# Gate projections of two row blocks formed together from seven block products each, in a Griffin-style trunk layer on one Trainium2 core

## The chip, the core and the metric

The kernel runs on one core of one Trainium2 chip. Its five engines run their own instruction streams and wait for each other through semaphores: PE (TensorE, matrix products into PSUM banks), DVE (VectorE), ACT (ScalarE), POOL (GpSimd), and SP (SyncE), which here issues most DMA transfers. The metric is the device time of one execution in microseconds; less is better.

## The reference

One layer over x of 2048 rows and 1024 channels, batch 1, float32 throughout. Only the projection concerns the change; the rest says what follows it.

```python
h = _rmsnorm(x, norm1_g[layer])
proj = jnp.einsum('bsd,de->bse', h, w_in[layer])
(a_q, a_k, a_v, b_q, b_lat, i_q, i_k, i_w, gate_a, gate_b) = _split_cols(proj)
o_a = _mixer_a(...)       # sliding-window attention, 8 heads
o_b = _mixer_b(...)       # indexer scores, top 256 keys per row, attention over them
merged = (jax.nn.sigmoid(gate_a) * jnp.einsum('bse,ed->bsd', o_a, w_branch_a[layer])
          + jax.nn.sigmoid(gate_b) * jnp.einsum('bse,ed->bsd', o_b, w_branch_b[layer]))
x = x + jnp.einsum('bsd,de->bse', merged, w_out[layer])
# then x + SwiGLU(RMSNorm(x)) and a final RMSNorm
```

gate_a and gate_b have 1024 columns each: 16 column tiles of 128, numbered 0 to 15 below.

## The kernel before, in words

The 2048 rows are cut into four row blocks of 512 (`ROWS`, `NB`). The program first projects block 0, then 1, 2 and 3; then it runs, block by block, the attention, the branches, the output projection and the feed-forward part. A **job** is one column tile of one block: eight depth tiles of 128, and for each of them three products, since every float32 operand is held as a high and a low part in the type that PE takes (`three`, L1102: high by high, high by low, low by high). A projection job is thus 24 matmuls of 128x128 by 128x512, summed in one of four PSUM banks that are taken in turn (`take`, L1089). The table `JOBS` (L385) sets the order: per block iq (4 jobs), ikw, lat, av, ak, aq (4), bq (4) and the 16 gate tiles; the list `SECOND` (L386) is the part from av on.

What is done for a job on each engine:

- SP loads its 512 KB of weights into one of two tiles `WRAW` (L861), in the order of `JOBS`. Before the load of job i it waits until POOL has split job i-2, and it issues, at fixed places of the same queue, what has to be written out or loaded meanwhile (`spill` L660, `first_attention` L819).
- POOL splits the weights, half a job (four depth tiles, 128x512) at a time: `WHI` by L1038 and `WLO` by L1040. The half of job i waits until PE is through with job i-2 (L1032), whose `WHI`/`WLO` it overwrites.
- PE runs the job (`job`, L1107).
- ACT and DVE take the bank away. For a gate tile ACT applies the sigmoid and writes the 256 KB to DRAM (L1939, L1941).

Where a new block begins, PE turns the normalised rows (`XN`) into columns, ACT writes their high part `HThi` (L1882) and DVE the low part `HTlo` (L2461), eight columns of 128x512 each; the first four are turned within the last job of the block before, the other four within the first job of the new block.

Beside the jobs run two more things. The indexer's scores: PE makes units of up to 128x1024 in PSUM (`score`, L1253), spread over the jobs from `SECOND`'s sixth on by `score_share` (L593); ACT applies the relu, DVE multiplies and adds (L2447). And the search for block 0's top keys (`search`, L2192): one step per job of `SECOND` in blocks 1 and 2, in which DVE sets thresholds and counts one row tile, and ACT counts another (L1849). The last two gate tiles of block 3 (`HELD`) are run within the first attention. The queries for it (`QA`) are loaded into the place of the indexer's keys, so SP waits for the last score (L834) before it issues that load, just ahead of the load of gate tile 12 of block 3.

The product of seven instead of eight block products is already used for the down projection of the last block (`seven_products`, L1189).

## Time and profile before

| what | us |
|---|---|
| three runs: median (lowest, highest) | 3185.56 (3185.35, 3195.97) |
| the profiled execution's own time | 3185.86 |
| its span in the profile | 3183.9 |
| PE busy, share of the span | 3143.7, 99% |
| POOL busy | 2059.9, 65% |
| DVE busy | 2005.0, 63% |
| ACT busy | 1449.8, 46% |

A busy time is the union of an engine's instructions; matmuls overlap their neighbours in it, so the time that one more matmul costs is the distance between two starts, not the duration of one. The projections take from the start to about 859 us; block 1 begins at 205 us.

### The profile page before, as it was taken

How to read it: one execution, taken by the hardware profiler on the slowest of the kernel's cores; microseconds unless marked ns; L12 is line 12 of the kernel's file. 1: busy time of each engine (PE TensorE's matmuls, PEld its weight loads, DVE VectorE, ACT ScalarE, POOL GpSimd, SP SyncE). 2: the span in 40 equal slices, each digit the busy share in tenths (PEclk: the TensorE clock that was granted, in tenths of full speed). 3: DMA queues.
4: the chain of work that ended last, by engine and by line, in shares of the span. 5: the costliest groups of instructions: out<-in, count | busy, mean ns of one | idle time of the engine just before them, and what ended most of it. 6: DMA issues, size and time to landing. Idle time of an engine off the chain costs nothing.

```text
span 3183.9 us, 44209 instructions
## 1 busy us (share of the span) xinstructions
PE 3143.7 (99%) x15612; PEld 2643.7 (83%) x15612; DVE 2005.0 (63%) x3889; ACT 1449.8 (46%) x2622; POOL 2059.9 (65%) x2185
## 2 busy tenths in 40 slices
PE   9999999999999999999999999999999999999998
PEld 7888888878888888889888888988888789888887
DVE  3235546537565545557666666967868679647757
ACT  3324445435472534337354543846655368431202
POOL 5666666665556666764666676366666932568778
PEclk9999999999999999999999999999999999999999
DMA  5765455355615333331633334163333411444443
GB/s 154 197 168 172 120 150 161 106 158 164 210 35 182 103 106 108 109 133 35 218 103 108 107 111 139 30 213 116 102 108 105 151 62 21 137 160 127 126 127 101
DMA packets 474699, 401.25 MB, mean 126 GB/s; under 512 B 29905, under 2 KB 405969, under 8 KB 473841
## 3 DMA queue, kind: packets, MB, share of 16 engines
q1 hardware_dynamic: 441072, 342.68, 35.9%
q10 hardware_dynamic: 33408, 55.76, 4.9%
q8 instruction: 126, 2.06, 0.3%
q14 instruction: 93, 0.75, 0.1%
HBM read 332.41 MB, written 62.81 MB: 124 GB/s over the span
## 4 chain that ended last, share of the span: by engine, by line
PE 92%; POOL 3%; ACT 2%; DVE 1%; issue 1%; DMA 1%; POOLq 0%; SPq 0%; ACTq 0%; DVEq 0%
PE BANK L1103 21%; PE BANK L1104 21%; PE BANK L1105 21%; PE BANK L1426 3%; PE LP L1103 3%; PE LP L1104 3%; PE LP L1105 3%; PE BANK L1451 2%; PE LP L1262 2%; PE LP L1261 2%; PE LP L1406 2%; PE LP L1407 2%; PE BANK L1453 2%; POOL WLO L1040 2%; POOL WHI L1038 1%; PE LP L1223 1%
## 5 line engine op out<-in xcount | busy, mean ns | idle before, releaser
L1040 POOL TENSOR_TENSOR WLO<-WRAW,WHI 128x512 fp32r<-128x512 f32 x904 | 1222.7, 1353 | 75.4
L1038 POOL TENSOR_SCALAR WHI<-WRAW 128x512 fp32r<-128x512 f32 x904 | 655.1, 725 | 736.5 <-PE BANK L1105 585.6
L1103 PE MATMUL BANK<-H2hi,WHI 128*128 128x512 f32 x1376 | 539.0, 392 | 1.0 <-POOL WLO L1040 0.9
L1104 PE MATMUL BANK<-H2lo,WHI 128*128 128x512 f32 x1376 | 536.2, 390 | 0.0
L1105 PE MATMUL BANK<-H2hi,WLO 128*128 128x512 f32 x1376 | 536.1, 390 | 0.0
L1103 PE MATMUL BANK<-HThi,WHI 128*128 128x512 f32 (+1 forms) x1024 | 405.4, 396 | 0.8 <-DVE QS L2183 0.5
L1104 PE MATMUL BANK<-HTlo,WHI 128*128 128x512 f32 (+1 forms) x1024 | 399.7, 390 | 0.0
L1105 PE MATMUL BANK<-HThi,WLO 128*128 128x512 f32 (+1 forms) x1024 | 399.5, 390 | 0.0
L1849 ACT ACTIVATE MASK<-SCD,THR 128x896 bf16<-128x896 f32 (+5 forms) x186 | 281.9, 1516 | 190.9 <-DVE THR L2243 164.3
L1105 PEld LDWEIGHTS BANK<-H2hi,WLO 128*128 128x128 f32 x1376 | 258.3, 188 | 54.2
L1103 PEld LDWEIGHTS BANK<-H2hi,WHI 128*128 128x128 f32 x1376 | 258.6, 188 | 53.1 <-issue 1.3
L1104 PEld LDWEIGHTS BANK<-H2lo,WHI 128*128 128x128 f32 x1376 | 258.6, 188 | 51.4
L2210 DVE TENSOR_SCALAR_CACHE_REDUCE MASK<-SCD,THR 128x640 bf16<-128x640 f32 (+2 forms) x192 | 278.1, 1486 | 3.4
L1837 ACT ACTIVATE RB<-LP 128x1024 f32<-128x1024 f32 (+7 forms) x176 | 143.4, 818 | 227.9 <-PE LP L1262 206.1
L2447 DVE SCALAR_TENSOR_TENSOR SCP<-RB,IW,SCP 128x1024 f32<-128x1024 f32 (+7 forms) x140 | 171.8, 1241 | 106.3 <-ACT RB L1837 105.2
L2376 DVE TENSOR_TENSOR PTlo<-BANK,PThi 128x512 fp32r<-128x512 f32 (+1 forms) x296 | 193.3, 659 | 57.8 <-ACT PThi L1778 56.5
L1105 PEld LDWEIGHTS BANK<-HThi,WLO 128*128 128x128 f32 (+1 forms) x1024 | 191.1, 187 | 42.8
L1103 PEld LDWEIGHTS BANK<-HThi,WHI 128*128 128x128 f32 (+1 forms) x1024 | 191.1, 187 | 38.8 <-issue 0.6
L1104 PEld LDWEIGHTS BANK<-HTlo,WHI 128*128 128x128 f32 (+1 forms) x1024 | 191.3, 187 | 36.9
L1731 ACT ACTIVATE LGb<-LGb,NMB 128x1024 f32<-128x1024 f32 (+7 forms) x192 | 174.1, 907 | 57.7 <-POOL NMB L959 55.0
L959 POOL TENSOR_SCALAR NMB<-MXB 128x1 f32<-128x1 f32 x112 | 32.3, 289 | 252.5 <-DVE MXB L2333 244.0
L1778 ACT CAST PThi<-BANK 128x512 fp32r<-128x512 f32 (+1 forms) x296 | 164.0, 560 | 50.9 <-PE BANK L1426 46.8
(356 smaller groups left out, 6552.7 us busy)
## 6 DMA issues: line engine op xcount, KB each, us to landing
WRAW<-in_w_in SPq DMA_DIRECT2D x124, 512.0 KB, 4.3
WRAW<-in_w_ffn_gate SPq DMA_DIRECT2D x88, 512.0 KB, 3.9
WRAW<-in_w_ffn_up SPq DMA_DIRECT2D x88, 512.0 KB, 3.8
WRAW<-in_w_ffn_down SPq DMA_DIRECT2D x81, 512.0 KB, 3.7
qsp<-QS SPq DMA_DIRECT2D x32, 512.0 KB, 5.8
WRAW<-in_w_out SPq DMA_DIRECT2D x32, 512.0 KB, 4.6
gates<-GS ACTq DMA_DIRECT2D x62, 256.0 KB, 2.2
GL<-gates ACTq DMA_DIRECT2D x48, 256.0 KB, 4.0
```

The costliest lines, as they stand in the source:

```text
L1038: nc.gpsimd.tensor_scalar(hi, raw, 1.0, 1.0, ALU.mult, ALU.mult).then_inc(w_hi, 1)
L1040: nc.gpsimd.tensor_tensor(lo, raw, hi.bitcast(f32), ALU.subtract).then_inc(w_split, 1)
L1103: nc.tensor.matmul(dst, whi, mhi, start=first, stop=False)
L1104: nc.tensor.matmul(dst, whi, mlo, start=False, stop=False)
L1105: return nc.tensor.matmul(dst, wlo, mhi, start=False, stop=last)
L1731: nc.scalar.activation(lg, lg, ACT.Exp, bias=NMB[:, slot, 0:1], accum_out=(ES if s else RS)[:, j, h0:h0 + 1]).then_inc(probs, made(probs, ...
L1778: nc.scalar.copy(PTHI[b][r][:, 0:w, :], trans(key)[:, 0:w, :]).then_inc(pt_hi, made(pt_hi, key))
L1837: nc.scalar.activation(RB[:, g % 2, 0:w], logits(("idx",) + key)[:, 0:w], ACT.Relu).then_inc(relu_ready, made(relu_ready, key))
L1849: nc.scalar.activation(mask_of(b)[:, j, 0:w], found_at(b, j)[:, 0:w], ACT.Sign, bias=THR[:, j:j + 1].bitcast(f32), accum_out=CNT[:, j:j + ...
L2210: last = stepped(nc.vector.tensor_scalar(junk[:, j, 0:w], found_at(b, j)[:, 0:w], threshold(j), None, op, ALU.add, accum_out=CNT[:, j:j + 1]))
L2376: nc.vector.tensor_tensor(PTLO[b][r][:, 0:w, :], trans(key)[:, 0:w, :], PTHI[b][r][:, 0:w, :].bitcast(f32), ALU.subtract).then_inc(pt_read ...
L2447: ins = nc.vector.scalar_tensor_tensor(s, r, iw, s, ALU.mult, ALU.add)
```

## The change

For a pair of neighbouring row blocks (0 with 1, 2 with 3) and a pair of neighbouring gate tiles, the four jobs of 24 matmuls are replaced by seven products of 12 matmuls, a **unit**. The operand H is halved by row block (512 rows each) and by depth (columns 0 to 3 and 4 to 7), the weights by depth and by tile. Four of the seven products take sums of H halves (S1 to S4) and differences of weight halves (T0 to T3) in place of the halves themselves, as in the Strassen-Winograd scheme. Six units (12 tiles) are formed for blocks 0 and 1 and run in block 1; four units (8 tiles) for blocks 2 and 3 run in block 3. The other gate tiles stay jobs as before, some ahead of the units (`GATES_AHEAD`), some at the end (`GATES_BEHIND`).

What that takes on the engines:

- SP copies H of block 0 (and 2) to free places in SBUF, four DMA transfers of 1 MB (`keep_columns`); it loads two weight tiles per unit.
- ACT writes the columns of block 1 (and 3) a second time, whole, over `XN` (`raw_column`), makes the high parts of S1 to S4, copies three partial products per unit out of PSUM, and applies the sigmoids.
- DVE makes S1 to S4 and their low parts (22 operations of 128x1024 per block), four differences of 128x512 and three additions per unit.
- POOL splits seven halves per unit in place of eight.
- The scores begin at `SECOND`'s second entry and lie in fewer jobs; `LAG`, the distance at which SP writes results out, goes from 6 to 4; in blocks 1 and 3 the reload of x and some loads for the attention move to other places of SP's queue.

The core of the diff:

```diff
+        UNITS = (6, 4)
+        GATES_AHEAD = ((), (12, 13, 14), (), (8, 9, 10))
+        GATES_BEHIND = ((12, 13, 14, 15), (15,), tuple(range(8, 16)), (11, 12, 13, 14, 15))
+        OPERAND = ("a11", "a12", 1, 2, 0, "a22", 3)
+        WEIGHT = ("b11", "b21", 1, 2, 0, 3, "b22")
+        INTO_BANK = ("gx", "gy", "gx", "gz", "gx", "gz", "gx")
...
-            first, end = 5, len(SECOND) - 2 if b + 1 < NB else len(SECOND) - 8
+            first, end = 1, len(SECOND[b]) - (2 if b + 1 < NB else 6)
...
+                    if dst is A11[b // 2][0]:
+                        sp.wait_ge(va_out, n(va_out, b))
+                        sp.wait_ge(kb_out, n(kb_out, (b, 1)))
...
-            LAG, PROJ = 6, NB * len(projections(0))
+            LAG, PROJ = 4, sum(len(projections(b)) for b in range(NB))
...
+            def paired_gates(b):
+
+                left = dict(a11=A11[b // 2], a12=A12, a22=(HThi[:, 4:8, :], HTlo[:, 4:8, :]))
+                for u in range(UNITS[b // 2]):
+                    for m in range(7):
+                        i, a = job_no[0] + (7 * u + m) // 2, (7 * u + m) % 2
+                        which, into = OPERAND[m], INTO_BANK[m]
+                        if STARTS[m]:
+                            release = (gate_ready, (b - 1, 2 * u + 1)) if into == "gx" else (gate_summed, (b, u, "c11" if into == "gy" else "c21"))
+                            take("bank", *release, (into, b, u))
+                        elif m == 2:
+                            pe.wait_ge(half_kept, n(half_kept, (b, u, "p1")))
...
+                        else:
+                            pe.wait_ge(gate_summed, n(gate_summed, (b, u, "c22")))
...
+                        for s in range(4):
+                            if u == 0 and type(which) is int and s % 2 == 0:
+                                pe.wait_ge(sum_low, n(sum_low, (b, which, s // 2)))
...
+                for u in range(UNITS[b // 2]):
+                    gates = pair_gates(b, u)
+                    keep(u, 0, "p1", 0)
+                    summed(u, "c11", gates[0], 0)
+                    keep(u, 2, "u2", 1)
+                    keep(u, 3, "z", 2)
+                    if u == 0:
+                        sum_high(b, 3)
+                    summed(u, "c22", gates[1], 2)
+                    if b == 1:
+                        next(early, None)
+                    summed(u, "c21", gates[2], 1)
+                    act.wait_ge(bank_full, n(bank_full, product_key(b, 7 * u + 6)))
+                    store_gate(*gates[3], GS[:, GATES.index(gates[3]) % 2, :], bank(("gx", b, u))[:, :])
+                    if b == 1:
+                        next(early, None)
```

Three places of the instruction streams show the change. The first is DVE at the start of block 1, before: the low parts of the eight columns, and then the first job's query heads.

```order
L2461 SCALAR_TENSOR_TENSOR HTlo<-LP,G_72,HThi 128x512 [waits h_hi] x8
L2183 SCALAR_TENSOR_TENSOR Q<-BANK,Q 64x512 [waits q_hi,bank_full]
L2183 SCALAR_TENSOR_TENSOR Q<-BANK,Q 64x512
L2183 SCALAR_TENSOR_TENSOR Q<-BANK,Q 64x512 [waits q_hi,bank_full]
L2183 SCALAR_TENSOR_TENSOR Q<-BANK,Q 64x512
```

The same place now (SRAW are the unsplit sums S1 to S4, A11 the kept first four columns of block 0, TW the weight differences T0 to T3). Where DVE had eight operations ahead of the first job's results it now makes three of the four sums, two low parts and four differences behind them.

```order
L2777 SCALAR_TENSOR_TENSOR HTlo<-LP,G_72,HThi 128x512 [waits h_hi] x8
L2686 TENSOR_TENSOR SRAW_150<-A11hi_134,A11lo_135 128x1024 [waits ak_out,columns_kept]
L2686 TENSOR_TENSOR SRAW_150<-A11hi_134,A11lo_135 128x1024
L2730 TENSOR_TENSOR SRAW_148<-XN 128x4x2x128 [waits raw_kept] x2
L2686 TENSOR_TENSOR SRAW_149<-SRAW_148,SRAW_150 128x1024 [waits sum_made] x2
L2739 TENSOR_TENSOR SRAW_150<-SRAW_150,XN 128x4x2x128 [waits sum_made] x2
L2700 TENSOR_TENSOR S2lo<-SRAW_149,S2hi 128x1024 [waits sum_hi] x2
L2715 TENSOR_TENSOR TW<-WRAW_51,WRAW_52 128x512 [waits w_loaded0,w_loaded1,sum_made]
L2715 TENSOR_TENSOR TW<-WRAW_51,TW 128x512 [waits sum_made]
L2715 TENSOR_TENSOR TW<-WRAW_51 128x512
L2715 TENSOR_TENSOR TW<-WRAW_52,TW 128x512 [waits sum_made]
L2700 TENSOR_TENSOR S3lo<-SRAW_150,S3hi 128x1024 [waits sum_hi] x2
```

The second place is DVE within the first unit of block 1, behind the addition of c11 and the first call of the search: the rest of the sums and the first unit's c22 (GPART_157). All of the fourth sum lies ahead of the c22 addition, for which PE's seventh product waits.

```order
L2700 TENSOR_TENSOR S1lo<-SRAW_148,S1hi 128x1024 [waits sum_hi] x2
L2686 TENSOR_TENSOR SRAW_151<-A12hi,A12lo 128x1024 [waits ftab_out]
L2686 TENSOR_TENSOR SRAW_151<-A12hi,A12lo 128x1024
L2686 TENSOR_TENSOR SRAW_151<-SRAW_151,S2hi 128x1024 [waits sum_made] x2
L2686 TENSOR_TENSOR SRAW_151<-SRAW_151,S2lo 128x1024 [waits sum_made] x2
L2700 TENSOR_TENSOR S4lo<-SRAW_151,S4hi 128x1024 [waits sum_hi] x2
L2721 TENSOR_TENSOR GPART_157<-BANK,GPART_157 128x512 [waits half_kept,bank_full]
L2458 TENSOR_SCALAR TAKE<-CNT 128x1 [waits topk_step]
L2462 TENSOR_SCALAR TAKE<-CNT 128x1 [waits tiles_counted]
L2465 SCALAR_TENSOR_TENSOR THR<-TAKE,THR 128x2 [waits topk_step]
L2432 TENSOR_SCALAR MASK_124,CNT<-SC_104,THR 128x384 [waits threshold_set]
L2715 TENSOR_TENSOR TW<-WPAIR_153,WPAIR_152 128x512 [waits w_split,w_loaded0,w_loaded1]
```

The third place is SP's queue at the end of block 3, before: the loads of gate tiles 10 to 12 (WRAW), with `QA` ahead of gate tile 12's.

```order
L861 DMA WRAW_51<-in_w_in 128x8x128 [waits w_split]
L696 DMA scd<-SCP 128x1792 [waits score_ready]
L861 DMA WRAW_52<-in_w_in 128x8x128 [waits w_split]
L729 DMA QA<-qsp 128x2x1024 [waits logits_full]
L729 DMA QA<-qsp 128x2x1024
L861 DMA WRAW_51<-in_w_in 128x8x128 [waits w_split]
L721 DMA KBhi<-kbd 128x512
L721 DMA KBlo<-kbd 128x512
L724 DMA VB_137<-vbd 128x512
```

The same place now: the first two WRAW loads are those of gate tiles 11 and 12. `QA` still stands ahead of gate tile 12, with the write-outs of queries, keys and values now close before it, and the score for which it waits is now two jobs ahead of gate tile 12's job on PE, where it was four.

```order
L945 DMA WRAW_51<-in_w_in 128x8x128 [waits w_split]
L696 DMA qsp<-QS_1_133 128x1024 [waits q_ready]
L725 DMA kbd<-KBShi 128x512 [waits k_ready]
L725 DMA kbd<-KBSlo 128x512
L728 DMA vbd<-VBS 128x512 [waits v_ready]
L771 DMA QA<-qsp 128x2x1024 [waits vb_out,logits_full,kb_out,va_out]
L771 DMA QA<-qsp 128x2x1024
L945 DMA WRAW_52<-in_w_in 128x8x128 [waits w_split]
L696 DMA qsp<-QS_0_132 128x1024 [waits q_ready]
L763 DMA KBhi<-kbd 128x512
L763 DMA KBlo<-kbd 128x512
L766 DMA VB_164<-vbd 128x512
```

## Rows read from the trace of the kernel before

**Rows 1.** The page, part 1: each engine's busy time, share of the span, instructions.
```profile
PE 3143.7 (99%) x15612; PEld 2643.7 (83%) x15612; DVE 2005.0 (63%) x3889; ACT 1449.8 (46%) x2622; POOL 2059.9 (65%) x2185
```

**Rows 2.** Timeline of PE in block 0: start us, duration us, engine, line, operation.
```profile
28.73 0.39 PE L1103 MATMUL BANK<-HThi,WHI 128*128 128x512 f32 x1
...
34.17 0.39 PE L1103 MATMUL BANK<-HThi,WHI 128*128 128x512 f32 x1
```

**Rows 3.** The same view where block 1 begins: its first job and its second.
```profile
205.13 0.60 PE L1275 MATMUL LP<-IDENT,XN 128*128 128x128 f32 x4
...
212.39 0.39 PE L1103 MATMUL BANK<-HThi,WHI 128*128 128x512 f32 x1
```

**Rows 4.** Timeline of ACT at the same place.
```profile
205.33 0.60 ACT L1939 ACTIVATE GS<-BANK 128x512 f32<-128x512 f32 x1 [1.33 <-PE BANK L1105]
...
206.33 1.27 ACT L1882 ACTIVATE HThi<-LP,G 128x512 fp32r<-128x512 f32 x2 [0.40 <-ACT GS L1939]
```

**Rows 5.** Answers by source line: ns minimum/median/maximum of one, first and last start.
```profile
L2672 DVE TENSOR_TENSOR TLO<-TRAW,THI x22: 1220/1634/2312, 2884.7 to 3142.4; 128x1024 fp32r<-128x1024 f32 x22
...
L2513 DVE TENSOR_TENSOR LTlo<-LT,LThi x4: 691/1086/1480, 72.5 to 690.3; 128x512 fp32r<-128x512 f32 x4
...
L2461 DVE SCALAR_TENSOR_TENSOR HTlo<-LP,G,HThi x32: 740/750/752, 13.4 to 638.5; 128x512 fp32r<-128x512 f32 x32
...
L1038 POOL TENSOR_SCALAR WHI<-WRAW x904: 432/620/2590, 11.9 to 3166.9; 128x512 fp32r<-128x512 f32 x180, 128x288 fp32r<-128x288 f32 x1
...
L1040 POOL TENSOR_TENSOR WLO<-WRAW,WHI x904: 802/1292/3186, 12.7 to 3167.6; 128x512 fp32r<-128x512 f32 x180, 128x288 fp32r<-128x288 f32 x1
```

**Rows 6.** Timeline of POOL late in block 0.
```profile
186.66 1.29 POOL L1040 TENSOR_TENSOR WLO<-WRAW,WHI 128x512 fp32r<-128x512 f32 x1
187.91 1.06 POOL L1038 TENSOR_SCALAR WHI<-WRAW 128x512 fp32r<-128x512 f32 x1
```

**Rows 7.** Timeline of DVE at the same moment.
```profile
186.97 1.52 DVE L2447 SCALAR_TENSOR_TENSOR SC<-RB,IW,SC 128x512 f32<-128x512 f32 x1 [4.37 <-ACT RB L1837]
```

**Rows 8.** Timeline of DVE: first call of block 0's search, then one step.
```profile
237.17 0.55 DVE L2210 TENSOR_SCALAR_CACHE_REDUCE MASK<-SC 128x384 bf16<-128x384 f32 x1
...
240.03 0.08 DVE L2210 DVE_READ_ACCUMULATOR MASK<-SC,THR 128x1 f32 x1
...
252.07 0.14 DVE L2236 TENSOR_SCALAR TAKE<-CNT 128x1 int32<-128x1 f32 x1
...
253.04 0.08 DVE L2210 DVE_READ_ACCUMULATOR MASK<-SC,THR 128x1 f32 x1
```

**Rows 9.** Groups of ACT by shape: count, busy us, mean ns, idle before.
```profile
L1939 ACT ACTIVATE GS<-BANK 128x512 f32<-128x512 f32 x62 | 36.7, 592 | 33.1 <-PE BANK L1105 33.0
...
L1849 ACT ACTIVATE MASK<-SC,THR 128x512 bf16<-128x512 f32 x31 | 22.2, 715 | 2.5 <-DVE THR L2243 1.9 <-ACT GS L1939 0.4
...
L2069 ACT CAST THI<-TRAW 128x1024 fp32r<-128x1024 f32 x22 | 22.0, 1048 | 0.0
```

**Rows 10.** Timeline of PE at the start of the attention; idle time in brackets.
```profile
873.52 0.35 PE L1391 MATMUL LP<-AKhi,QA 128*128 128x192 f32 x1 [2.53 <-DVE MX L2303]
```

**Rows 11.** Windows of 5 us there: busy us per engine, granted clock, DMA.
```profile
875.00:880.00 5.00, 5.00 (x24) 4.82 (x23) 4.20 (x20) 3.22 (x12) 0.54 (x3) 0.50 0.00 0
```

**Rows 12.** Timeline of SP's DMA issues before the attention.
```profile
831.79 0.88 SPq L729 DMA_DIRECT2D QA<-qsp  x2
836.86 0.37 SPq L861 DMA_DIRECT2D WRAW<-in_w_in  x1
```

**Rows 13.** DMA issues from 740 to 960 us: KB each, median us to landing.
```profile
QA<-qsp SPq DMA_DIRECT2D x2, 1024.0 KB, 7.1
...
kbd<-KBShi SPq DMA_DIRECT2D x1, 256.0 KB, 5.5
```

**Rows 14.** Groups of DVE by shape.
```profile
L2447 DVE SCALAR_TENSOR_TENSOR SCP<-RB,IW,SCP 128x1024 f32<-128x1024 f32 x70 | 99.6, 1422 | 71.3 <-ACT RB L1837 71.1
...
L2183 DVE SCALAR_TENSOR_TENSOR QS<-BANK,QS 64x512 fp32r<-64x512 f32 x64 | 44.1, 688 | 68.4 <-ACT QS L1650 66.7 <-PE BANK L1105 0.3
```

More of the change, by code:

```diff
@@ new lines, in load_pair @@
+            def load_pair(b, u):
+                first = FIRST_PRODUCT[b]
+                for t in range(2):
+                    s = w_in_sem[(first + t) % 2]
+                    if u == 1:
+                        sp.wait_ge(sum_made, n(sum_made, (b, "s3", 1)))
+                    if u:
+                        sp.wait_ge(s, n(s, ("pair", b, u - 1)))
+                    elif t:
+                        sp.wait_ge(w_split, 2 * first)
+                    made(s, ("pair", b, u), 16)
+                    dst = WPAIR[1][t] if u % 2 else WRAW[(first + t) % 2]
+                    sp.dma_start(dst[:, :, :], weights(w_in, range(KT), COL["gate"] + (2 * u + t) * P)).then_inc(s, 16)
@@ L855, in _ @@
                 if i >= 2:
                     sp.wait_ge(w_split, 2 * (i - 1))
+                if src is None:
+                    ahead = i - FIRST_PRODUCT[key[1]]
+                    for u in range(UNITS[key[1] // 2]):
+                        if ahead == (0, 2)[u] if u < 2 else ahead == (7 * (u - 1) + 1) // 2 + 1:
+                            load_pair(key[1], u)
+                    continue
+                k, width = src.shape[1], src.shape[2]
+                made(w_in_sem[i % 2], i, 16)
@@ L1308, in project @@
                     turn_first()
+                for m in GATES_AHEAD[b]:
+                    if m == GATES_AHEAD[b][0]:
+                        job(HThi, HTlo, (gate_ready, (b, m)), ready=(h_split, (b, 0)), beside=turn_more)
+                    else:
+                        job(HThi, HTlo, (gate_ready, (b, m)))
+                if b % 2:
+                    paired_gates(b)
                 for m in range(ET):
-                    if m == 0:
+                    if m == 0 and b % 2 == 0:
                         job(HThi, HTlo, (q_ready, (b, "iq", m, 1)), ready=(h_split, (b, 0)), beside=turn_more)
@@ L1882, in high_column, with raw_column, columns @@
                 nc.scalar.activation(HThi[:, k, :], bk[:, :], ACT.Copy, scale=G1[:, k:k + 1]).then_inc(h_hi, made(h_hi, (b, 0, k)))
+            def raw_column(b, k):
+                act.wait_ge(h_split, n(h_split, (b, 0, k)))
+                nc.scalar.activation(XN[:, :, k * P:(k + 1) * P], in_tiles(bank(("xt", b, k))), ACT.Copy, scale=G1[:, k:k + 1]
+                                     ).then_inc(raw_kept, made(raw_kept, (b, k)))
+            def columns(b, ks):
+                for k in ks:
+                    high_column(b, k)
+                    if b % 2 and k > ks[0]:
+                        raw_column(b, k - 1)
+                if b % 2:
+                    raw_column(b, ks[-1])
@@ new lines, in store_gate, with plain_gate @@
+            def store_gate(b, m, value, src):
+                g = GATES.index((b, m))
+                if g >= 2:
+                    act.wait_ge(gate_out[g % 2], 16 * (g // 2))
+                nc.scalar.activation(value, src, ACT.Sigmoid).then_inc(gate_ready, made(gate_ready, (b, m)))
+                act.wait_ge(gate_ready, n(gate_ready, (b, m)))
+                act.dma_start(io["gates"][b, m], value).then_inc(gate_out[g % 2], 16)
+            def plain_gate(b, m):
+                bk = full(("gate", b, m))
+                store_gate(b, m, GS[:, GATES.index((b, m)) % 2, :], bk[:, :])
@@ L1887, in project @@
                     act.wait_ge(const_first, 48)
-                for k in range(4 if b else 0, KT):
-                    high_column(b, k)
+                columns(b, range(4 if b else 0, KT))
+                if b % 2:
+                    paired_gates(b)
                 if b == 0:
```

280 lines of the change are left out of this document (231 added, 49 removed).

## Prediction

> **What bounds the kernel now.** I read the page's engine totals first: PE is busy 99% of the span, every other engine 65% or less [rows 1]. The reader is to see there that PE is the limit nearly everywhere, so a matmul taken away is worth its time, and that any wait put in front of PE costs in full. Then PE's timeline inside block 0: two jobs of 24 matmuls start 5.44 us apart, 0.2267 us per matmul [rows 2]; the 0.39 us shown for one matmul is no price, since neighbours overlap. After that I read the two ends of the change: block 1's start on PE and ACT [rows 3, 4], and the cost of vector work that will stand there [rows 5 to 9]; last, what PE does after a wait [rows 10, 11], SP's queue before the attention [rows 12, 13] and the score groups [rows 14].
>
> The sum is made against the profiled execution's own 3185.86 us, 0.3 us above the median of the three runs. A measurement of this kernel can tell about 0.5% from no change: 15.9 us, so faster means under 3169.9 and slower over 3201.8.
>
> **The change, part by part.**
>
> *Matmuls removed.* A unit has 7 products of 12 matmuls where four jobs had 96: 12 fewer, 120 in ten units. 120 x 0.2267 [rows 2] = **-27.2 us**, all on PE's path: 3158.7 if everything else hides. That the change does not do what it says I rule out: PE's instruction list is shorter by just these 120.
>
> *The sums, in the first unit of blocks 1 and 3.* This decides. PE's seventh product waits for the c22 addition, and DVE has all four sums, their low parts and the first four weight differences in its queue ahead of that. DVE is free for it from the last low part of the columns, about 212.1 in block 1, just before the second job starts [rows 3]; ACT's columns, 0.64 us each [rows 4] and now written twice, run beside the first job and delay this by perhaps 0.4 us. From there to the seventh product PE has 0.3 us of the first job, two gate jobs (10.9) and six products of 2.72 (16.3): **27.5 us**. DVE has 22 operations of 128x1024. The nearest row is the last block's subtraction of that shape, 1.22 us at its shortest [rows 5]: 26.8. Add four differences of 128x512 at 0.69 (shortest of the like row [rows 5]), 2.8; two additions from PSUM, 0.7 each by the low parts' 0.75 [rows 5], 1.4; and in block 1 a first search call, 2.95 [rows 8]. Together 34.0 in block 1, 31.0 in block 3: even undisturbed, 6.5 and 3.5 late. That is the lower bound, 10 for both.
>
> It will be disturbed. At 186.66 POOL runs a WLO of 1.29 us; DVE's operation with two SBUF inputs starts at 186.97 and lasts 1.52, ending about 0.55 after WLO, and the WHI that follows takes 1.06 instead of its usual 0.62 [rows 5 to 7]. The two engines take turns. The low parts of the columns, which read PSUM beside POOL, always take 0.75 [rows 5], so it is the two-input SBUF operations that suffer, and those are nearly all of this list. In the 27.5 us POOL must split nine halves: two of the last gate job and seven products, 0.62 + 1.29 = 1.91 each [rows 5], 17.2 us. In turns: 26.8 + 2.8 + 17.2 + 0.7 (one addition on the way) = 47.5, 20 late; with two further halves that start before the chain ends, 24. I take 19 in each block, a little under the serial value because some splits fall into DVE's own waits for ACT's high parts: **+38 us** for both, between 10 and 48.
>
> The Trainium skill, "SBUF — State Buffer", section "SBUF: two separate sides", speaks against the change here: a DVE operation with two SBUF inputs and a GpSimd operation exclude each other for the whole instruction, instead of sharing bandwidth. The trace agrees (1.52 us where about 0.6 would do). By that rule the sum ends where I put it; if the two only shared mildly, it would be rival B.
>
> *The later units of block 1.* From the fourth product's end the chain is: c22 addition 0.7; sigmoid 0.59 [rows 9] and its DMA issue, about 0.4 (an estimate from the 0.4 us gap after such a store [rows 4]); ACT's search count 0.72 [rows 9]; DVE's step 1.05 [rows 8]; four differences 2.8 with one POOL half between, 1.9; c21 addition 0.7; sigmoid and issue 1.0; the last sigmoid 0.6; together about 10.5, 11 with semaphore steps. That sigmoid frees the bank with which the next unit's second product, or its fourth, is formed; the four products after it take 10.9. So a period of 22.0 against PE's 7 x 2.72 = 19.05: 2.9 at five boundaries would be 15. I take **+12** (0 to 15). Block 3 has no search in its units: **+2** (0 to 3).
>
> *The clock.* After PE waits 2.53 us at the start of the attention [rows 10], the next window stands at granted clock 0.50, the 1.2 GHz level [rows 11]; 24 matmuls fill 5 us there where 22 x 0.2267 would: I estimate about 3 us lost per long wait. Three waits of that kind are new (two sums, gate tile 12): **+9** (0 to 25).
>
> *SP's queue in block 3.* `QA` now waits for a score that ends about two jobs before gate tile 12's job instead of four, and that tile's weights are queued behind 2 MB of `QA`, whose landing takes 7.1 us [rows 12, 13]. From the score's release T the weights land at about T + 9 to 11 and their split takes 1.9 more; PE, with one job and the rest of a job ahead, wants them near T + 6.3. **+6** (3 to 10).
>
> *Block 0.* The last copy of H waits for a write-out just issued (5.5 us to land [rows 13]) and its 1 MB lies ahead of gate tile 13's weights: **+2** (0 to 5).
>
> *Denser scores.* In block 3, 58 units now lie in 8 jobs, 7.25 each: 7.25 x 1.42 = 10.3 on DVE plus two query operations 1.4 [rows 14] = 11.7, against PE's 5.44 + 7.25 x 4 x 0.2267 = 12.0. It holds by 0.3, before POOL's turns: **+2** (0 to 6). In block 1 the units are half as many: nothing.
>
> *At nothing:* POOL's splits for ten halves fewer (POOL is 65% busy [rows 1]); the copies and pair loads of SP otherwise, under jobs whose weights are prefetched two deep; the search, whose 41 calls still exceed the 37 it needs. If that cover went, one missing prefetch costs about a landing of 5.5 to 7 us [rows 13].
>
> Sum: -27.2 + 38 + 12 + 2 + 9 + 6 + 2 + 2 = +43.8, against 3185.9: **3230 us**.
>
> **The rivals.**
>
> A, the forecast: the first units late by some 15 to 24 each, small losses elsewhere. With the first-unit term between 25 and 48 and half the spread of the rest, 3204 to 3262.
>
> B, DVE is not slowed by POOL, and only the 10 us of its own excess is late. -27.2 + 10 + 5 + 3 + 6 + 2 + 2 = +0.8: **3187**. For it: the low parts beside POOL lose nothing [rows 5]. Against it: they read PSUM; the two-input row does lose [rows 7], and the median of the 128x1024 row is 1.63, not 1.22 [rows 5].
>
> C, the other side: the sums are ready in time, and nothing replaces the removed work. DVE would need 22 x 1.0 + 2.8 + 1.4 = 26.2, under 27.5. The point from which it decides is 1.06 us per operation with POOL's halves in DVE's waits. For it: the 1.22 row writes the split type, and half of the 22 write plain float32, perhaps quicker; ACT's high parts of 1.05 [rows 9] leave DVE gaps. Then the time is 3158.7 + 3 for gate tile 12: **3162** (3158 to 3172), faster. Against it: nothing of that shape with two SBUF inputs is under 1.22 [rows 5].
>
> D, PE falls to the low clock at every new wait, first units at their upper bound, later units losing 15 and their clock: -27.2 + 48 + 15 + 3 + 20 + 10 + 5 + 5 = +78.8; with not all at once, **3265** (3255 to 3275). For it: a 2.5 us wait sufficed [rows 10, 11]. Against it: PE works densely between these waits.
>
> **How the numbers follow.** A 0.52, B 0.16, C 0.18, D 0.14. A, the two-engine turn-taking, has rows on its side but its price is worked out, not seen; C keeps more than its rows alone give, because A rests on the sums' price alone. Range: 3165 to 3268 leaves out most of C below (0.12) and part of D above (0.07); the forecast's own range is 3204 to 3262. Faster by over 0.5%: most of C, 0.16. Within 0.5%: B's and the rest of C, 0.18. Slower: A and D, 0.66.
>
> **What would show it.** PE idle before the seventh product of the first unit in blocks 1 and 3, some 15 us or more in all with earlier short waits at its third and fifth product, released by DVE's S4lo or GPART; DVE's 128x1024 operations at about 2 us beside POOL and 1.2 alone; a unit period near 22 us in block 1 and 19 to 20 in block 3; 0.50 clock windows after the long waits; PE idle before gate tile 12 in block 3, released by POOL after a late load. Wrong: products 3 to 7 of the first units back to back (then C), or DVE at 1.2 us with POOL at work beside it (then B); the removed 27.2 us should be seen in any case, as a distance of 2.72 us between products that wait for nothing.

## The result, and the profile after

| | us |
|---|---|
| before, median of the runs beside it | 3185.45 |
| changed kernel, median of four runs (lowest, highest) | 3263.37 (3259.66, 3264.27) |
| ratio, 95% interval | 1.0234, 1.0212 to 1.0257 |
| profiled execution: span before, after | 3183.9, 3257.8 |

The change makes the kernel slower, by 78 us between the medians. (The ratio of the two medians, 1.0245, lies within the interval of the ratio on record.) The forecast was 3230, with 3165 to 3268 as the range: slower, as said, but the time lies 33 us above the forecast and 1.4 us above the forecast's own range of 3204 to 3262.

The page of the changed kernel, part 1, against [rows 1]:

```profile
PE 3149.3 (97%) x15492; PEld 2634.0 (81%) x15492; DVE 2124.8 (65%) x4003; ACT 1488.0 (46%) x2680; POOL 2059.6 (63%) x2165
```

PE has 120 matmuls fewer and yet 2 points less of a longer span. Where the 74 us are, windows from one block turn to the next tell (from the first transposed row tile of a block to that of the next, the last up to the first attention). The columns are the window, its length, busy us of PE, PEld, DVE, ACT and POOL, the granted clock, the DMA share and GB/s. Before:

```profile
8.44:199.23 190.79, 189.41 (x865) 154.46 (x866) 66.09 (x80) 58.31 (x102) 127.47 (x130) 1.00 0.63 171
199.23:406.06 206.83, 206.83 (x954) 170.59 (x953) 111.86 (x215) 90.32 (x155) 137.78 (x129) 1.00 0.52 147
406.06:627.85 221.79, 221.79 (x1018) 182.44 (x1017) 131.04 (x187) 101.18 (x164) 140.11 (x129) 1.00 0.48 141
627.85:858.79 230.94, 229.36 (x1052) 188.95 (x1051) 126.74 (x124) 99.12 (x128) 139.83 (x123) 1.00 0.57 174
```

After:

```profile
8.42:141.86 133.44, 126.41 (x577) 101.73 (x578) 54.08 (x78) 48.08 (x88) 78.16 (x82) 0.97 0.74 210
141.86:430.18 288.32, 266.03 (x1170) 213.65 (x1169) 179.90 (x260) 114.05 (x189) 185.36 (x165) 0.98 0.38 112
430.18:629.14 198.96, 183.57 (x825) 147.96 (x826) 138.26 (x205) 100.77 (x165) 109.79 (x97) 0.97 0.49 150
629.14:930.61 301.47, 275.38 (x1196) 221.77 (x1195) 180.94 (x177) 123.48 (x164) 171.19 (x147) 0.95 0.45 139
```

By PE's work alone a stage should have changed by 5.44 us per job and 2.72 us per product:

| stage | jobs, products | should last | lasts | lost |
|---|---|---|---|---|
| block 0 | -12 | 190.8 - 65.3 = 125.5 | 133.4 | 7.9 |
| block 1 | -12, +42 | 206.8 - 65.3 + 114.2 = 255.8 | 288.3 | 32.5 |
| block 2 | -8 | 221.8 - 43.5 = 178.3 | 199.0 | 20.7 |
| block 3 | -8, +28 | 230.9 - 43.5 + 76.2 = 263.6 | 301.5 | 37.9 |

Lost are 99 us, saved 27; the rest of the program is 2 us longer. No stage is without a loss, block 2 neither, in which nothing is paired. The table of PE's waits (us in total, times, longest) names them:

```profile
PE LP L1383 <- DVE XN L2394: 15.0, 6, 5.3
PE BANK L1211 <- POOL WLO L1124: 13.9, 4, 6.6
PE BANK L1433 <- DVE GPART L2721: 13.1, 2, 7.7
PE LP L1369 <- ACT RB L1986: 12.1, 16, 1.6
PE BANK L1433 <- issue: 5.3, 4, 2.1
PE BANK L1433 <- DVE S1lo L2700: 4.0, 1, 4.0
PE BANK L1433 <- ACT GS L2055: 3.8, 5, 0.9
PE BANK L1433 <- POOL WLO L1146: 3.3, 5, 0.8
```

L1433 are the products. GPART and S1lo are the first units' waits for the sums; L1146 and nearly all of "issue" are their waits for POOL's split of the weights, which takes turns with DVE's sums; GS is the later units' wait in block 1. L1211 are plain jobs whose weights came late (above all gate tile 13 of block 0 and gate tile 12 of block 3). Not forecast were the first line, the rows of the next block at the three block turns, and the size of the fourth, the scores' banks (L1369: PE waits until ACT has taken earlier scores out). Before, the same table had no wait for the rows at these turns, and for the scores' banks:

```profile
PE LP L1261 <- ACT RB L1837: 1.6, 1, 1.6
```

**The first unit.** PE's timeline in block 1, third, fifth and seventh product:

```profile
178.96 0.47 PE L1433 MATMUL BANK<-S2hi,WHI 128*128 128x512 f32 x1 [2.12 <-issue]
189.69 0.77 PE L1433 MATMUL BANK<-S1hi,WHI 128*128 128x512 f32 x1 [3.96 <-DVE S1lo L2700]
203.49 0.80 PE L1433 MATMUL BANK<-S4hi,WHI 128*128 128x512 f32 x1 [5.41 <-DVE GPART L2721]
```

The "issue" ahead of the third product is POOL's split of the weight difference, which ends at 178.86:

```profile
177.29 1.57 POOL L1146 TENSOR_TENSOR WLO<-TW,WHI 128x512 fp32r<-128x512 f32 x1
```

And DVE's list ahead of the seventh, from its first operation to the c22 addition:

```profile
157.33 2.35 DVE L2686 TENSOR_TENSOR SRAW<-A11hi,A11lo 128x1024 f32<-128x1024 f32 x2
159.59 3.87 DVE L2730 TENSOR_TENSOR SRAW<-XN 128x1024 f32<-128x1024 f32 x2
...
181.42 0.68 DVE L2721 TENSOR_TENSOR GPART<-BANK,GPART 128x512 f32<-128x512 f32 x1
...
183.32 1.30 DVE L2443 TENSOR_SCALAR TAKE<-CNT 128x2 int32<-128x2 f32 x1
...
187.70 3.40 DVE L2700 TENSOR_TENSOR S1lo<-SRAW,S1hi 128x1024 fp32r<-128x1024 f32 x2
...
202.75 0.68 DVE L2721 TENSOR_TENSOR GPART<-BANK,GPART 128x512 f32<-128x512 f32 x1
```

Two operations take 2.35 us where POOL is idle and 3.87 where it splits: 1.2 and 1.9 each. The list lasts 46.1 us (157.33 to 203.43), without a gap in it; 5.8 us of it are the search's first call (182.02 to 187.78).

**The turn into block 2.** DVE, then PE:

```profile
427.55 7.49 DVE L2667 SCALAR_TENSOR_TENSOR SCP<-RB,IW,SCP 128x1024 f32<-128x1024 f32 x4
435.11 0.11 DVE L2672 MEMSET SCP<- 64x64 f32 x1
435.15 0.68 DVE L2394 TENSOR_SCALAR XN<-XN,SS 128x1024 f32<-128x1024 f32 x1
```

```profile
435.88 0.47 PE L1383 MATMUL LP<-IDENT,XN 128*128 128x128 f32 x1 [5.27 <-DVE XN L2394]
439.08 0.48 PE L1383 MATMUL LP<-IDENT,XN 128*128 128x128 f32 x1 [2.72 <-DVE XN L2394]
```

DVE scales one row tile of the next block per entry of `SECOND`, behind that entry's scores, query heads and search step. With 11 entries in block 1 instead of 26 it has no time between them: the operation that PE needs takes 0.68 us and stands behind 7.5 us of scores.

**The clock** around this wait, in windows of 2 us (columns as above):

```profile
432.00:434.00 2.00, 0.00 (x0) 0.00 (x0) 1.90 (x2) 1.98 (x5) 1.96 (x1) 1.00 0.01 4
436.00:438.00 2.00, 0.36 (x1) 0.06 (x1) 1.90 (x5) 0.81 (x2) 0.00 (x0) 0.50 0.00 0
440.00:442.00 2.00, 2.00 (x8) 1.60 (x8) 0.75 (x1) 0.56 (x2) 0.00 (x0) 0.50 0.89 185
446.00:448.00 2.00, 2.00 (x13) 1.65 (x12) 0.75 (x1) 1.97 (x3) 0.39 (x1) 1.00 0.71 286
```

PE stands idle, the granted clock falls to 0.50, the 1.2 GHz level, within the wait, and from 446 on, some 5 us after work begins again, it is back at 1.00. With this one, low clock is seen at eight new places: gate tile 13 of block 0, fifth and seventh product of block 1's first unit, the turns into blocks 2 and 3, third and seventh product of block 3's first unit, gate tile 12 of block 3. In them matmuls of 512 columns start 0.43 us apart instead of 0.2267; the excess over the usual distances, all matmuls of a stretch counted, is 1.7 to 3.0 us in each and 20.9 us in all.

### The profile page after: what moved, and what is told of

It reads as the page before. It is cut to its first block, busy times and chain, and to the rows that moved or that the text cites. A ratio compares the mean times of both kernels' runs of the same rounds, so it can differ in the third digit from the quotient of the medians.

```text
span 3257.8 us, 44267 instructions
## 1 busy us (share of the span) xinstructions
PE 3149.3 (97%) x15492; PEld 2634.0 (81%) x15492; DVE 2124.8 (65%) x4003; ACT 1488.0 (46%) x2680; POOL 2059.6 (63%) x2165
## 3 DMA queue, kind: packets, MB, share of 16 engines
q1 hardware_dynamic: 421424, 340.58, 34.3%
## 4 chain that ended last, share of the span: by engine, by line
PE 80%; DVE 8%; ACT 4%; POOL 3%; issue 3%; DMA 1%; ACTq 0%; SPq 0%; POOLq 0%; DVEq 0%
PE BANK L1211 17%; PE BANK L1212 16%; PE BANK L1213 16%; PE BANK L1575 3%; PE LP L1211 3%; PE LP L1212 3%; PE LP L1213 3%; PE BANK L1600 2%; PE LP L1555 2%; PE LP L1556 2%; DVE SCP L2667 2%; PE BANK L1602 2%; POOL WLO L1124 2%; DMA WRAW<-in_w_in 1%; PE BANK L1433 1%
## 5 line engine op out<-in xcount | busy, mean ns | idle before, releaser
L1124 POOL TENSOR_TENSOR WLO<-WRAW,WHI 128x512 fp32r<-128x512 f32 (+1 forms) x824 | 1121.0, 1360 | 68.8
L1122 POOL TENSOR_SCALAR WHI<-WRAW 128x512 fp32r<-128x512 f32 (+1 forms) x824 | 592.5, 719 | 755.0 <-PE BANK L1213 540.3
L1211 PE MATMUL BANK<-H2hi,WHI 128*128 128x512 f32 x1376 | 538.7, 392 | 1.0 <-POOL WLO L1124 0.9
L1211 PEld LDWEIGHTS BANK<-H2hi,WHI 128*128 128x128 f32 x1376 | 258.5, 188 | 53.2 <-issue 1.3
L1211 PE MATMUL BANK<-HThi,WHI 128*128 128x512 f32 (+1 forms) x704 | 284.8, 404 | 12.9 <-POOL WLO L1124 12.9
L1212 PE MATMUL BANK<-HTlo,WHI 128*128 128x512 f32 (+1 forms) x704 | 278.1, 395 | 0.0
L1213 PE MATMUL BANK<-HThi,WLO 128*128 128x512 f32 (+1 forms) x704 | 277.8, 395 | 0.0
L2667 DVE SCALAR_TENSOR_TENSOR SCP<-RB,IW,SCP 128x1024 f32<-128x1024 f32 (+7 forms) x140 | 177.1, 1291 | 33.4 <-ACT RB L1986 29.9
L1575 PE MATMUL BANK<-IDENT,LGb 128*128 128x128 f32 x1088 | 164.1, 273 | 3.7 <-ACT LGb L1880 1.9
L1211 PEld LDWEIGHTS BANK<-HThi,WHI 128*128 128x128 f32 (+1 forms) x704 | 133.2, 189 | 39.7 <-issue 14.6
L1600 PE MATMUL BANK<-PThi,VB 128*128 128x256 f32 x544 | 154.3, 305 | 5.7 <-DVE PTlo L2598 2.9
```

What stands on the lines that cost most here:

```text
L1122: nc.gpsimd.tensor_scalar(hi, raw, 1.0, 1.0, ALU.mult, ALU.mult).then_inc(w_hi, 1)
L1124: nc.gpsimd.tensor_tensor(lo, raw, hi.bitcast(f32), ALU.subtract).then_inc(w_split, 1)
L1211: nc.tensor.matmul(dst, whi, mhi, start=first, stop=False)
L1212: nc.tensor.matmul(dst, whi, mlo, start=False, stop=False)
L1213: return nc.tensor.matmul(dst, wlo, mhi, start=False, stop=last)
L1575: last = nc.tensor.transpose(dst[:, 2 * e + h, :], probabilities(b, kind, p, h, t), IDENT[:, :])
```

## The experiments

The theory after the result: each wait in the table costs its own length, the low clock behind it comes from the idle PE, and three things make the waits: DVE's list for the first unit, lengthened by POOL's splits; DVE's order in shortened stages; and transfers ahead of weights on SP's queue. Each edit below is made on the changed kernel unless it says otherwise. Gains are differences of medians; the unchanged kernel's median beside the runs moved between 3185.5 and 3187.1, so a gain is good to about 2 us.

**Rows of the next block earlier** (ACT's squares and root one entry earlier too):

```diff
+                    to_go = len(SECOND[b]) - s
+                    if b + 1 < NB and 3 <= to_go <= 6:
+                        next(scaled)
                     for _ in range(score_share(b, s)):
                         next(todo)
-                    to_go = len(SECOND[b]) - s
-                    if b + 1 < NB and to_go == 7:
+                    if b + 1 < NB and to_go == 8:
                         scaled = scaled_rows(b + 1)
-                        next(scaled)
-                    if b + 1 < NB and 2 <= to_go <= 5:
                         next(scaled)
```

> The next block's rows are scaled one job earlier, and ahead of that job's scores in DVE's queue instead of behind them (squares and root on ACT one job earlier too). In the changed kernel PE waits 15.0 us for XN in six waits at the three block turns, and the granted clock is low behind two of them (20 us windows at 0.83 and at 0.86/0.89, together about 8 us lost). Theory, the order in DVE's queue: the waits for XN go (under 2 us left) and with them the low clock, 3263 - 23 = about 3240 us. Rival, DVE is simply full in block 1 (18 to 19 of each 20 us from 360 to 440): at the turn into block 2 the 8.7 us come back as waits for the scores' banks, only the turns into blocks 1 and 3 gain (7 us and one 3.4 us clock dip), about 3253 us.

Measured: 3249.36, ratio 1.0196 (1.018 to 1.0211): 14 us back, between the two and nearer to the second. All six waits for XN are gone. But PE's timeline at the turn into block 2 has a new one:

```profile
440.57 0.63 PE L1383 MATMUL LP<-IDENT,XN 128*128 128x128 f32 x4 [3.84 <-DVE HTlo L2777]
```

The low parts of the columns now wait behind the same scores and search steps, and the waits for the scores' banks rise from 12.1 to 15.6 us. Both theories hold in part: at the turns into blocks 1 and 3 it was the order, at the end of block 1 DVE is full.

**Copies of H behind the weight load**:

```diff
-                if i < PROJ and key[1] % 2 == 0:
-                    keep_columns(key[1], key)
...
                 sp.dma_start(raw, src).then_inc(w_in_sem[i % 2], 16)
+                if i < PROJ and key[1] % 2 == 0:
+                    keep_columns(key[1], key)
```

> The copies of H of blocks 0 and 2 are issued behind the weight load of the same step instead of ahead of it. Theory, SP's queue: the load of gate tile 13 no longer stands behind a wait for the key write-out; PE's waits of 1.58 us (82.5) and 4.73 us (126.0) in block 0 go, and the low clock behind the second (3.4 us): 3263 - 9.7 = about 3254 us. Rival, bandwidth: the 1 MB copies slow the next weights as much wherever they are issued, so the wait moves to the next gate tile and less than 4 us is gained.

Measured: 3256.63, ratio 1.022 (1.0205 to 1.0236): 6.7 us back. The 4.73 us before gate tile 13 are gone with the low clock behind them; the smaller wait stays (83.5, 1.91 us) and another of its kind comes one gate tile later:

```profile
130.73 0.47 PE L1211 MATMUL BANK<-HThi,WHI 128*128 128x512 f32 x1 [1.91 <-POOL WLO L1124]
```

Mostly the wait in SP's queue, then. The 1 MB still stands ahead of the next load, and whether the remainder is its place in the queue or bandwidth this run does not tell apart.

**QA later**:

```diff
-                if t == 28:
+                if t == 30:
                     sp.wait_ge(va_out, n(va_out, NB - 1))
...
                     load_queries(0, "a", 1)
-                if t == 29:
+                if t == 30:
                     for k in range(3):
                         load_keys(0, k)
```

> The 2 MB of QA and the keys behind it are loaded two steps later on SP's queue, behind the weights of gate tiles 12 and 13 of block 3. Theory: PE's wait of 6.62 us before gate tile 12 goes, and the low clock behind it (about 3.4 us): 3263 - 10 = about 3253 us. Rival: the first attention then waits for QA, keys or the weights of the held gate tiles, and the time stays within 3 us of 3263.

Measured: 3260.73, ratio 1.0233 (1.0218 to 1.0248): 2.6 us, the rival; the lowest and highest of the two kernels are the same to 0.4 us. Block 3 is 10.2 us shorter by its stage (291.3), and what follows it 11.9 us longer. SP's issues, then PE:

```profile
910.32 1.20 SPq L771 DMA_DIRECT2D QA<-qsp  x2
...
913.85 0.51 SPq L945 DMA_DIRECT2D WRAW<-in_w_in  x1
```

```profile
929.97 0.77 PE L1211 MATMUL BANK<-HThi,WHI 128*128 128x512 f32 x1 [8.25 <-POOL WLO L1124]
```

The wait is only handed on, to a held gate tile in the first attention, and grows from 6.62 to 8.25 us. Everything that waited for the last score (2 MB of QA, keys, scores to be written out) still lies ahead of some weights.

**Search out of the first unit**: in both engines' `paired_gates`, `if b == 1:` ahead of a search call becomes

```diff
-                    if b == 1:
+                    if b == 1 and u:
                         next(early, None)
```

> The two search calls of the first unit of block 1 are left to later entries. The first call took 5.8 us of DVE in the chain (182.0 to 187.8; 2.95 us where it ran alone before the change). Theory, one serial chain on DVE up to the seventh product: it ends about 5.8 us earlier, the 3.96 us wait for S1lo goes, the seventh product still waits some 5 us: 3263 - 6 = about 3257 us, a little less if the clock dip behind the S1lo wait goes too (about 2.5 us are inside the chain and gain nothing). Rival, the chain is bound by the turns with POOL, not by DVE's own list: the sums then meet POOL's splits that ran beside the search's small operations, and only about 3 us are gained.

Measured: 3267.34, ratio 1.0256 (1.0239 to 1.0273): 4 us slower. In block 1 the wait for S1lo is gone and the stage is 3.0 us shorter (285.3): the rival's size, since S1lo and the A12 sum met POOL's splits instead (the c22 addition ends 43.6 us after the list's start, not 40.3). But block 2 lost 10.8 us. SP, PE:

```profile
615.34 0.50 SPq L904 DMA_DIRECT2D A11lo<-HTlo  x1
615.88 11.38 SPq L945 DMA_DIRECT2D WRAW<-in_w_in  x3
```

```profile
625.06 0.77 PE L1211 MATMUL BANK<-HThi,WHI 128*128 128x512 f32 x1 [11.48 <-POOL WLO L1124]
```

The copy of the low half of H of block 2 may only start when the search's masks are done, and weights stand behind it on SP's queue. In the changed kernel that copy is issued at 605.1, in time; two search calls later it comes at 615.3, and PE waits 11.5 us. The cover that the prediction counted at nothing was thinner than two calls.

**PE kept busy in its waits**:

```diff
+            def feed(dst, key):
+                for _ in range(FEED.get(key, 0)):
+                    nc.tensor.matmul(dst[:, 0:P], ONES[:, :], ONES[:, :], start=True, stop=True)
```

> Where PE waits over 1.3 us in the changed kernel (gate tile 13 of block 0, XN at the three turns, the fifth and seventh product of the first units, gate tile 12 of block 3) it now runs needless 128x128 matmuls of 0.15 us, a little shorter in sum than the wait; nothing else changes. The low clock stretches of the changed kernel add 17.8 us to the distances of the matmuls in them, 2.9 of it inside the first unit's chain of block 1, where it costs nothing. Theory, the clock falls because PE stands idle: the granted clock stays at 1.00 and 3263 - 15 = about 3248 us. Rival, the low clock has another cause (or the waits grow by the filling): granted clock as before, 3263 us or more.

Measured: 3261.69, ratio 1.0233 (1.0218 to 1.0248). The mean granted clock rose from 0.988 to 0.997, but the filling outlasted the waits; ahead of the seventh product of block 1 48 needless matmuls (two rows each in the trace) took

```profile
198.15 10.88 PE L1216 MATMUL LP<-ONES 128*128 128x128 f32 x96
```

where 7.1 us were free (the c22 addition ended at 205.24). So with two thirds of it:

> The filling once more, with two thirds of the needless matmuls: one of them takes 0.23 us, not the 0.15 that the filling before was counted with, so that it outlasted the waits by some 18 us in sum. Theory, the clock falls because PE stands idle: granted clock 1.00 and 3263 - 15 = about 3248 us. Rival, filling never gains: 3261 us or more, as in the run before.

Measured: 3255.58, ratio 1.0216 (1.0201 to 1.0231): 7.8 us back, half of what was expected. The window of the turn into block 2 shows that the clock stays (compare 436 to 438 above):

```profile
436.00:438.00 2.00, 1.91 (x17) 1.91 (x18) 1.87 (x8) 0.81 (x2) 0.00 (x0) 1.00 0.00 0
```

That the clock falls because PE is idle is shown: at the seven of the eight places that are filled it stays at 1.00, and at the third product of block 3's first unit, which is not filled, it falls as before. What it costs in all is less than the excess of the slow matmuls, and how much less is not shown place by place. One part lay beside another wait: in block 1 the seventh product now runs at full speed, and the next unit waits that much longer for the bank (0.22 us before):

```profile
209.68 0.50 PE L1446 MATMUL BANK<-A12hi,WHI 128*128 128x512 f32 x1 [2.80 <-ACT GS L2068]
```

**POOL out of the first units' way**:

```diff
+                    if u == 0:
+                        raw, hi, lo = (t[:, 0:1, 0:2] for t in (raw, hi, lo))
                     nc.gpsimd.tensor_scalar(hi, raw, 1.0, 1.0, ALU.mult, ALU.mult).then_inc(w_hi, 1)
```

> Leaves out POOL's splits of the first unit's seven products in blocks 1 and 3 (POOL touches two elements per half instead of 128x512, so the products use what weights lie there). Theory, DVE and POOL take turns on SBUF: without them DVE's 128x1024 operations take 1.2 us instead of 1.9, the list up to the seventh product some 35 us instead of 46.1 in block 1 and 33 instead of 43.6 in block 3 (the last gate tile's splits stay), 3263 - 21 to 25 = about 3240 us. Rival, DVE's operations are slow by themselves (split-type output, two SBUF inputs, strided rows): they stay at 1.9 us and the time at 3260 or more.

Measured: 3243.63, ratio 1.0179 (1.0164 to 1.0194): 19.7 us back, the theory. DVE's low part of the third sum, by tile (ns minimum/median/maximum), changed kernel and then this one:

```profile
L2700 DVE TENSOR_TENSOR S3lo<-SRAW,S3hi x4: 1624/1952/2277, 177.7 to 670.4; 128x1024 fp32r<-128x1024 f32 x4
```

```profile
L2702 DVE TENSOR_TENSOR S3lo<-SRAW,S3hi x4: 1217/1218/1219, 174.5 to 659.1; 128x1024 fp32r<-128x1024 f32 x4
```

The seventh product's waits are still 8.0 and 6.3 us: PE comes there earlier, and DVE's list of 37.7 us (157.6 to 195.3), in part still beside splits of the last gate tile and of the second unit, is longer than PE's work, as the lower bound had it.

**One pair of blocks alone** (blocks 2 and 3 back to plain jobs):

```diff
-        UNITS = (6, 4)
-        GATES_AHEAD = ((), (12, 13, 14), (), (8, 9, 10))
-        GATES_BEHIND = ((12, 13, 14, 15), (15,), tuple(range(8, 16)), (11, 12, 13, 14, 15))
+        UNITS = (6, 0)
+        GATES_AHEAD = ((), (12, 13, 14), (), ())
+        GATES_BEHIND = ((12, 13, 14, 15), (15,), tuple(range(16)), tuple(range(16)))
```

> Only blocks 0 and 1 are paired (six units); blocks 2 and 3 compute their 16 gate tiles as plain jobs. By the stages of the changed kernel's trace, counted against the matmuls of each: block 3 loses 37.9 us and saves 10.9, and of block 2's 20.7 us some 11 are the turn at its start. Theory, the losses lie where they are seen: without the second pair about 27 + 10 = 37 us come back, 3263 - 37 = about 3226 us, still slower than before. Rival, the second pair's losses are carried over from the first (search steps displaced from block 1, scores closer together): less than 25 us come back, over 3238 us.

Measured: 3224.67, ratio 1.0117 (1.0101 to 1.0134): 38.7 us back. The two pairs make the kernel slower by about the same, 37.5 us the first and 38.7 the second. Of the first pair's, about 10 lie at the start of block 2, where the rows come late (block 2 lasts 231.9 us, 221.8 before).

**The first pair mended**: on the kernel of the run before, the rows earlier and the copies behind as above, no search call in the first unit, one per later unit, none in block 1's other entries, and instead:

```diff
-                    if b in (1, 2):
+                    if b == 2 or b == 3 and s < 10:
                         next(early, None)
```

> The pair of blocks 0/1 alone, with the rows scaled earlier, the copies behind the weight loads, and the search moved: none in the first unit, one call per later unit, none in block 1's other entries, the rest in blocks 2 and 3. Theory, losses are where the trace shows them and add up: from 3225, rows 10 to 12, copies 6, search out of the first unit and the later units' chain 4 + 5, less load on DVE at the end of block 1 some 3: about 3195 us, slower than before by 0.3%. Rival, DVE and the shared port stay full and each mended wait comes back at the next place: 3210 us or more.

Measured: 3195.9, ratio 1.0033 (1.002 to 1.0046): 28.8 us back, the theory to 1 us. Block 2 lasts 221.35 us and PE has no wait at its start any more; the later units' waits for GS are gone too. The longest wait left in block 1 is that of the first unit's seventh product:

```profile
195.70 0.80 PE L1434 MATMUL BANK<-S4hi,WHI 128*128 128x512 f32 x1 [7.68 <-DVE GPART L2720]
```

**A shorter list for the sums**, on top of that: H of block 0 is put together at the end of block 0, and S4 is taken from S2 before S2 is split.

```diff
+                    if b == 0 and to_go == 3:
+                        early_sums(1)
...
+                    made_sum(3, h, SRAW[3][:, c, :], SRAW[1][:, c, :], ALU.subtract, "s4")
...
-                            made_sum(3, h, SRAW[3][:, c, :], SUMS[1][0][:, c, :].bitcast(f32), ALU.subtract, "s4hi")
...
-                            made_sum(3, h, SRAW[3][:, c, :], SUMS[1][1][:, c, :].bitcast(f32), ALU.subtract, "s4")
```

> As the run before, and the sums of the first unit of block 1 take 16 operations of 128x1024 in the list ahead of the seventh product instead of 22: H of block 0 is put together again at the end of block 0 (4), and the fourth sum is taken from the second before that is split (2 fewer). Theory, the list decides: six operations of 1.2 to 1.9 us less, 3195 - 8 = about 3187 us, no different from before. Rival, the operations only move to a place where POOL is as busy and the rows and scores wait for them: less than 3 us gained.

Measured: 3187.26, ratio 1.0003 (0.9993 to 1.0012): 8.6 us back. DVE's list:

```profile
155.03 2.35 DVE L2736 TENSOR_TENSOR SRAW<-XN 128x1024 f32<-128x1024 f32 x2
157.29 7.66 DVE L2696 TENSOR_TENSOR SRAW<-SRAW,SRAW 128x1024 f32<-128x1024 f32 x4
...
188.62 0.68 DVE L2731 TENSOR_TENSOR GPART<-BANK,GPART 128x512 f32<-128x512 f32 x1
```

It lasts 34.3 us (155.03 to 189.30), and the seventh product no longer waits. Block 1 is 8.9 us shorter. The four operations moved to block 0 are not free there: a half that POOL splits beside them takes 3.45 us instead of 1.99, PE waits 2.13 us where the run before had no wait, and block 0 is 2.1 us longer (133.7 for 131.6):

```profile
140.04 0.47 PE L1212 MATMUL BANK<-HThi,WHI 128*128 128x512 f32 x1 [2.13 <-POOL WLO L1125]
```

**Smaller copies**: the copies of H in eight pieces of 512 KB over eight steps, and the weight differences ahead of S2's low part.

```diff
+                at_ = [("ak", b, 0), ("aq", b, 0), ("aq", b, 1), ("aq", b, 2), ("aq", b, 3), ("bq", b, 0), ("bq", b, 3), ("gate", b, 13)]
...
-                lower_sum(1)
                 dve.wait_ge(sum_made, n(sum_made, (b, "s3", 1)))
                 sum_weights(0)
+                lower_sum(1)
```

> As the run before, with the copies of H of block 0 issued as eight of 512 KB over eight steps, and the first unit's weight differences taken ahead of the second sum's low part. PE still waits 6.7 us before four jobs of block 0 and 2.1 us before the first unit's third product in the run before. Theory, a 512 KB copy ahead of a load delays it by half as much and hides under the two jobs of prefetch, and POOL's split of the difference runs beside DVE's low part: 3187.3 - 6 = about 3181 us, 0.15% faster than before. Rival, the transfers of block 0 fill the queues whatever their size, and POOL and DVE take turns there too: less than 2 us gained.

Measured: 3184.48, ratio 0.9992 (0.9983 to 1.0001): 2.8 us back, half of what was expected; not to be told from before. Block 0 gained 4.5 us by its stage (133.7 to 129.2), block 1 nothing (265.7 and 266.2). Most of what six units save, 16.3 us, is spent again on what is left: by the stages 3.7 us in block 0 and 10.4 in block 1.

## Why the prediction was right, and where its sum was too small

*Matmuls, -27.2.* Right: in block 3 the later units follow each other every 19.04 us (their second product starts at 699.74, 718.78 and 737.82), 84 x 0.2267.

*Sums of the first units, +38.* The mechanism was right, the size 5 us too high. The list in turns was forecast at 47.5 us for either block, with no search call in it; it took 46.1 us in block 1, 5.8 of them the search, and 43.6 in block 3, which has no search there. The seventh product came 17.8 and 15.2 us later than behind gapless products, 33.0 for 38 (block 1: 203.49 against 169.42 + 16.3). The run without POOL's splits shows the turns: 1.95 us for an operation beside POOL, 1.22 without. It also shows how strict they are. POOL's operation on two elements took 1.16 us beside a low part of 1.2 us (S3lo) and 0.19 beside DVE's addition from PSUM:

```profile
174.65 1.16 POOL L1146 TENSOR_SCALAR WHI<-TW 128x2 fp32r<-128x2 f32 x1
...
176.92 0.19 POOL L1146 TENSOR_SCALAR WHI<-TW 128x2 fp32r<-128x2 f32 x1
```

The Trainium skill, "SBUF — State Buffer", section "SBUF: two separate sides", has this as an exclusive lock for the whole instruction; two elements that wait for a full DVE operation agree with that, and not with shared bandwidth. Rival B is out.

*Later units, +12 and +2.* The chain is the one that was named (the search between c22 and c21, then the sigmoid that frees the bank), but a period is 20.23 us in block 1 instead of 22.0, and 19.04 in block 3: 5 and 0 us. With the call behind c22 taken out the waits for GS vanish.

*The clock, +9.* The price of one place came out about right (1.7 to 3.0 us of excess where 3 was estimated), but by luck: 24 matmuls in 5 us, where 22 x 0.2267 would fill them, show no loss, and most of those 24 have fewer than 512 columns. The number of places was wrong, eight for three, 20.9 us. How much of that is net stays open: the run with fewer needless matmuls gave 7.8 us back.

*SP's queue in block 3, +6.* Measured 6.6. The reason was right as well: it is the transfers behind the last score, and moving QA does not help.

*Block 0, +2.* Measured 6.3 (1.58 and 4.73), above the bound of 5: the bound took one landing, but SP, waiting for the key write-out of 108.98 to land, issued nothing between 111.84 and 115.06, and then 1 MB ahead of the weights.

*Denser scores, +2.* This step failed. The text worked out block 3, where the waits for the scores' banks, 3.5 us, stayed within its 0 to 6; of block 1 it said "the units are half as many: nothing", and block 2 it did not look at. In blocks 0, 1 and 2 the query heads, the scores, the next block's rows and (in 1 and 2) the search steps share 14, 11 and 18 entries where they had 26, and the rows stand last in each. That made 15.0 us of waits for XN, 3.1, 8.0 and 3.9 at the turns into blocks 1, 2 and 3. The waits for the scores' banks are 12.1 us instead of 1.6, but only 1.2 of them lie in block 1, and 7.4 in block 2; what makes them there no run separates. The rows of the next block, which no term named, are the largest single miss. Measured together 25.5 us for 2.

*At nothing.* No later unit waits for POOL's splits or for the pair loads; the first units do wait for splits, within the term of the sums. The search's place cost nothing in the changed kernel, but with little to spare: SP's copy in block 2 hangs on it, as the run with two calls moved shows.

The terms as measured, -27.2 + 33.0 + 5 + 20.9 + 6.6 + 6.3 + 25.5, make 70.1; the slow stretches of the fifth product of block 1 (2.8) and the third of block 3 (1.7) are in it twice, and the remaining 8 of the 74 us of the spans are in gaps too small for a line here. By stage, waits and slow stretches make 8.6 of the 7.9 us lost in block 0, 29.9 of 32.5, 18.4 of 20.7 and 37.6 of 37.9. This says where PE's time lies, not what each mend gives back. The measured time is that of rival D, and only in part for D's reason: low clock behind many new waits was right (20 us there, 20.9 of excess measured), but the first units stayed below the forecast's middle value, the later units lost 5 us and not 18, and the rest is work that lost its room. The range of 3204 to 3262 does not follow from the terms either: 13 below and 10 above for the sums, and half of the other terms' distances to their bounds, 15 and 15.5, give 3202 to 3256.

## What to carry to other kernels

Work for DVE with two SBUF inputs has to be counted against the time that POOL leaves on SBUF, not against DVE's idle share: a job of 5.44 us has 2 x 1.91 = 3.8 us of POOL's splits, which by this estimate leaves DVE 1.6 us if POOL is to keep its pace; 26.8 us of sums then need some 16 jobs of cover, and 27.5 us, about five jobs, were there. When jobs are taken out of a stage, count what every engine does per job beside them: the fixed work (scores, search, the next block's rows, transfers) moves closer together, and what stands last in an in-order queue is late first. A saving of under one per cent of PE's work (27.2 of 3144 us) is soon spent: mended at five places, the first pair came from 37.5 us slower to no difference.

## What was not expected of the hardware

Small operations on DVE wait for POOL as well: one operation of the search's first call, on 128x2 elements with a single SBUF input, took 1.30 us beside a split (183.32, above) and 0.17 in the run without splits, and the whole call 5.8 us instead of 2.95 [rows 8]. In the changed kernel the granted clock was 0.50 behind each of PE's waits of 2.53 to 7.67 us; behind the third product's wait it stayed at 1.00 in block 1 (2.12 us) and was 0.50 in block 3 (2.10 us), so the length of a wait alone does not tell. A needless 128x128 float32 matmul costs 0.23 us (48 in 10.88 us), as much as one of 512 columns in the split type.
